# Summing the squares of a norm block by block between the tiles of the product before it

## What is computed

```python
def _rms(x, w):
    y = x * lax.rsqrt(jnp.mean(x * x, axis=-1, keepdims=True) + EPS)
    return y * w

for l in range(DEPTH):                                  # DEPTH = 2
    h = _rms(x, norm1_w[l]) * (1 + sc1) + sh1           # norm "n1"
    y = token_mixers(h)          # ends in mix @ w_o[l]: eight tiles of 128 outputs
    x = x + g1 * y
    h = _rms(x, norm2_w[l]) * (1 + sc2) + sh2           # norm "n2"
    f = swiglu(h) if l == 0 else moe(h)   # the dense one ends in a @ w_down: eight tiles
    x = x + g2 * f
```

## Time and profile before

| | us |
|---|---|
| median of 3 runs | 1893.72 |
| lowest, highest | 1891.28, 1897.60 |
| the profiled execution, device time | 1892.12 |
| its span in the trace | 1890.1 |
| PE busy in the span | 1731.4 |
| PE weight loads busy | 1536.9 |
| DVE busy | 1356.2 |
| ACT busy | 1091.5 |

### The profile page before, as it was taken

How to read it: one execution, slowest core, us unless ns; L and a number is a source line. 1 busy time by engine, 2 the same in 40 slices (tenths; PEclk the granted TensorE clock), 3 DMA queues, 4 the chain that set the end, 5 groups by cost and what they waited for, 6 DMA issues and landing times.

```text
span 1890.1 us, 33664 instructions
## 1 busy us (share of the span) xinstructions
PE 1731.4 (92%) x11984; PEld 1536.9 (81%) x11984; DVE 1356.2 (72%) x2228; ACT 1091.5 (58%) x1837; POOL 39.4 (2%) x47
## 2 busy tenths in 40 slices
PE   6997888999989887767999999999999999999995
PEld 3884457999978654556999999999999999999995
DVE  4477345454455754357889889898898988988985
ACT  4453324444344532245777777777777777777772
POOL 0000100000000000000000000000000000000000
PEclk8998898999989997688999999999999999999998
DMA  9651362445436314037999999999999999999993
GB/s 385 219 199 45 135 266 90 156 165 186 160 112 236 136 45 164 1 159 268 363 360 365 355 347 379 359 357 365 353 363 359 346 380 360 360 359 348 370 358 124
DMA packets 52272, 494.22 MB, mean 261 GB/s; under 512 B 6256, under 2 KB 6560, under 8 KB 11120
## 3 DMA queue, kind: packets, MB, share of 16 engines
q1 hardware_dynamic: 48000, 479.59, 67.3%
q0 software_dynamic: 3840, 12.57, 1.8%
q10 hardware_dynamic: 368, 1.19, 0.2%
HBM read 484.97 MB, written 8.35 MB: 261 GB/s over the span
## 4 chain that ended last, share of the span: by engine, by line
PE 86%; DVE 8%; ACT 3%; DMA 2%; issue 2%; DVEq 0%; SPq 0%; ACTq 0%; POOLq 0%
PE bank L1019 17%; PE bank L1004 11%; PE bank L1006 11%; PE bank L1005 11%; PE bank L582 7%; PE bank L584 7%; PE bank L583 7%; PE bank L618 3%; PE bank L1012 1%; PE bank L590 1%; PE bank L865 1%; PE bank L778 1%; PE bank L843 1%; PE bank L597 1%; PE bank L839 1%
## 5 line engine op out<-in xcount | busy, mean ns | idle before, releaser
L1983 DVE TENSOR_TENSOR w_lo<-xring,w_hi 128x1024 fp32r<-128x1024 f32 x448 | 528.7, 1221 | 94.3 <-ACT w_hi L1335 94.3
L1004 PE MATMUL bank<-w_hi,hg_hi 128*128 128x256 f32 x1792 | 510.2, 285 | 5.6 <-DVE w_lo L1983 2.9
L1006 PE MATMUL bank<-w_hi,hg_lo 128*128 128x256 f32 x1792 | 507.9, 283 | 0.0
L1005 PE MATMUL bank<-w_lo,hg_hi 128*128 128x256 f32 x1792 | 507.7, 283 | 0.0
L1335 ACT ACTIVATE w_hi<-xring 128x1024 fp32r<-128x1024 f32 x448 | 449.7, 1060 | 0.0
L1004 PEld LDWEIGHTS bank<-w_hi,hg_hi 128*128 128x128 f32 x1792 | 342.1, 191 | 17.9 <-DVE w_lo L1983 4.7
L1005 PEld LDWEIGHTS bank<-w_lo,hg_hi 128*128 128x128 f32 x1792 | 342.1, 191 | 7.5
L1006 PEld LDWEIGHTS bank<-w_hi,hg_lo 128*128 128x128 f32 x1792 | 342.3, 191 | 0.0
L1983 DVE TENSOR_TENSOR wd_lo<-xring,wd_hi 128x1024 fp32r<-128x1024 f32 x224 | 273.0, 1219 | 0.0
L1338 ACT ACTIVATE wd_hi<-xring 128x1024 fp32r<-128x1024 f32 x224 | 236.5, 1056 | 2.1 <-PEq L973 2.1
L1351 ACT ACTIVATE sgX<-bank 128x128 f32<-128x128 f32 x224 | 62.2, 278 | 252.2 <-PE bank L1006 252.2
(11 more groups left out here) (305 smaller groups left out, 2613.5 us busy)
## 6 DMA issues: line engine op xcount, KB each, us to landing
xring<-w_moe SPq DMA_DIRECT2D x224, 1536.0 KB, 8.6
ring<-w_ada SPq DMA_DIRECT2D x32, 1536.0 KB, 7.7
ring<-w_win SPq DMA_DIRECT2D x22, 1024.0 KB, 6.6
ring<-w_up SPq DMA_DIRECT2D x22, 1024.0 KB, 4.8
ring<-w_down SPq DMA_DIRECT2D x8, 1408.0 KB, 5.9
ring<-w_wo SPq DMA_DIRECT2D x8, 1024.0 KB, 6.3
ring<-w_wqb SPq DMA_DIRECT2D x2, 1152.0 KB, 8.6
ring<-w_wkvb SPq DMA_DIRECT2D x2, 1024.0 KB, 5.5
```

Source lines behind the costliest of these rows:

```text
L1004: mm(banks[j][:, 0:256], hg_hi[:, k], w_hi[:, j % 2, cols], start=k == 0, stop=False)
L1005: mm(banks[j][:, 0:256], hg_hi[:, k], w_lo[:, j % 2, cols], start=False, stop=False)
L1006: last = mm(banks[j][:, 0:256], hg_lo[:, k], w_hi[:, j % 2, cols], start=False, stop=k == KD - 1)
L1983: v.tensor_tensor(lo, xring[:, s + D * p:s + D * p + D], hi.bitcast(F32), ALU.subtract).then_inc(sem("lo_done"), 1)
```

## The change

`SS_LAG = 2` is new. On PE, block k - 2 of the sum of squares is multiplied right behind tile k, for k from 2 on; behind the last tile come the last three blocks. On ACT, the square of a block stands behind the rounding of a later tile's weights. The eight blocks accumulate in one bank, which is taken at tile 2 instead of after tile 7. In the bank plan the sum therefore comes at another place, and the n1 of layer 1 gets a stated bank (3) and no longer takes a turn. DVE, SP and POOL keep their instructions in their order.

```diff
@@ psum_plan
-        use(("ss", l, "n1"))
         if l == 0:
+            use(("ss", l, "n1"))
             ada(("start", 0))
...
         for k in range(KD):
             use(("wo", l, k))
-        use(("ss", l, "n2"))
+            if k == SS_LAG:
+                use(("ss", l, "n2"))
         if l == 0:
             plan["before the dense layer"] = list(count)
             for k in range(KD):
-                use(("down", k), (4 + k) % 8)
+                use(("down", k), (4 + k) % 8 if k < KD - 1 else 4)
+                if k == SS_LAG:
+                    use(("ss", 1, "n1"), 3)
@@ PE
-            def sum_x_squares(l, name):
-                o = use(("ss", l, name))
-                for k in range(KD):
+            def sum_x_squares(l, name, ks=range(KD)):
+                o = use(("ss", l, name)) if ks[0] == 0 else ps(("ss", l, name))
+                for k in ks:
                     pe.wait_ge(sem("x_squared"), KD * (2 * l + (name == "n2")) + k + 1)
                     last = mm(o[:, 0:T], ones, sq8_f[:, k * T:(k + 1) * T], start=k == 0, stop=k == KD - 1)
-                full(last, ("ss", l, name))
+                if ks[-1] == KD - 1:
+                    full(last, ("ss", l, name))
+
+            def sum_behind(l, name, k):
+                if k >= SS_LAG:
+                    sum_x_squares(l, name, range(k - SS_LAG, KD if k == KD - 1 else k - SS_LAG + 1))
...
                 for k in range(KD):
                     tile_product((NP + KD) * l + NP + k)
-                sum_x_squares(l, "n2")
+                    sum_behind(l, "n2", k)
...
                         full(last, ("down", k))
+                        sum_behind(1, "n1", k)
@@ ACT
                 for k in range(2, KD):
                     round_weights((NP + KD) * l + NP + k)
-                square_x(l, "n2", (sem("x1_ready"), KD * l))
+                    if k > SS_LAG:
+                        square_x(l, "n2", (sem("x1_ready"), KD * l), [k - SS_LAG - 1])
+                square_x(l, "n2", (sem("x1_ready"), KD * l), range(KD - SS_LAG - 1, KD))
...
                     for d in range(2, KD * DOWN_PIECES):
                         round_down_piece(d)
+                        if d >= SS_LAG * DOWN_PIECES and d % DOWN_PIECES == 1:
+                            square_x(1, "n1", (sem("ffn_x_ready"), 0), [d // DOWN_PIECES - SS_LAG])
```

More of the change, by code:

```diff
@@ L187 @@
 MLA_ORDER = mla_order()
+SS_LAG = 2
 def psum_plan():
@@ L629, in _ @@
                     modulation(("start0", 0))
-                sum_x_squares(l, "n1")
                 if l == 0:
+                    sum_x_squares(l, "n1")
                     modulation(("start", 0))
@@ L1087, in modulation_rows, with square_x @@
                     act.sem_inc(sem("modrow_ready"), 1)
-            def square_x(l, name, ready):
-                for k in range(KD):
+            def square_x(l, name, ready, ks=range(KD)):
+                for k in ks:
                     act.wait_ge(ready[0], ready[1] + k + 1)
                     A(sq8_f[:, k * T:(k + 1) * T], xT[:, k * T:(k + 1) * T], ACT.Square).then_inc(sem("x_squared"), 1)
-                act.sem_inc(squares_ready, 1)
+                if ks[-1] == KD - 1:
+                    act.sem_inc(squares_ready, 1)
             def shift_rounded(l, dst, col, k, signal):
@@ L1119, in _ @@
                     act.wait_ge(sem("eps_ready"), 1)
-                square_x(l, "n1", (sem("xT_ready"), 0) if l == 0 else (sem("ffn_x_ready"), 0))
                 if l == 0:
+                    square_x(l, "n1", (sem("xT_ready"), 0))
                     modulation_rows(("start0", 0))
+                else:
+                    square_x(l, "n1", (sem("ffn_x_ready"), 0), range(KD - SS_LAG, KD))
                 finish_norm(l, "n1", D)
```

## The result

| | before | after |
|---|---|---|
| median (lowest to highest), us | 1893.31 (1889.82 to 1897.60) | 1896.88 (1893.86 to 1901.24) |
| profiled execution, device time | 1892.12 | 1895.26 |
| its span | 1890.1 | 1893.2 |

The ratio is 1.0023 [1.0016, 1.0030], so the change costs 4.4 us (3.0 to 5.7); the medians differ by 3.6 us. That is within the 0.3% that a single measurement tells from no change. With 22 runs on each side it is a small, real loss, larger than the +1.8 us forecast. The runs of either kernel lie in two groups (before 18 up to 1894.0 us and 4 from 1895.8 on, after 15 up to 1898.2 and 7 from 1899.9 on), and their medians differ by 3.3 us in the lower groups and 3.5 in the upper ones. The two profiled executions differ by 3.1 us in both time and span, so their traces can account for most of it.

The account below looks back on a forecast made before the run. PE, busy 92% of the span, was taken as the bound. Both w_o places +1.9, down product -0.75 and bank wait +0.6 us gave +1.8, so 1895.5 us against the median of 1893.7; range 1890.0 to 1899.3 us.

Parts of the forecast that it names:

- The class: Whole kernel: no difference beyond 0.3%, 5.7 us; same was given 0.90, faster 0.05, slower 0.05.
- Tails: Sum of squares behind three products: logarithm 2.29 us after the tile's end instead of 4.14, 5.55 us saved in all.
- Blocks between tiles: Both w_o products: five blocks at 0.56 us each, less the 1.85 us shorter tail, +0.95 us per place.
- the edge: PE, switching between a block and fp32r tiles: 0 to 0.17 us extra per block, taken as 0.08.
- the modulation step: Nearest rows with fp32 matmuls after a tile: 0.09 us over pitch going over, 0.08 going back.
- Down product: Five blocks between pieces cost net 0.22 us each, less the 1.85 us shorter tail: -0.75 us.
- the weight hole: Down product, at tile starts: PE loses 0.34 us waiting for weights, which a block would fill.
- Bank plan: Layer 1: head 0's scores wait for ACT's copy of tile 21 from bank 4, +0.6 us, or 0 if hidden.
- Squares on ACT: ACT's squares in w_o and the down product fall into its waits and cost nothing on the path.
- The clock: PE restarts at half clock after idle time; shifted restarts were allowed 1 us either way.
- The signs that the prediction named for being wrong: w_o tiles keeping their 3.20 us pitch, an edge over 0.3 us, or a changed length of the expert part.

Follow-up runs that it names:

- a run of its own: The changed kernel with layer 1's projection given back its earlier PSUM banks; 1896.56 us, ratio 1.0011 to the kernel before.
- the direct remedy: The changed kernel plus four redundant matmuls keeping PE busy ahead of layer 1's router; 1897.86 us, ratio 1.0014 to the kernel before.
- the one trace with all of them: Kernel before with all three sums three tiles behind and redundant matmuls in seven PE waits; 1888.15 us, ratio 0.9979 to the kernel before.

## Why the prediction came out as it did

The class was right (no difference beyond 0.3%), the range held the median, and the sign of +1.8 us was right. The size was short by about 2.6 us of 4.4. That the sign came out right is mostly luck: the terms that the sum was made of came to +0.4 us, not +1.8, and a term that was only allowed for, either way, brought the rest.

- *Tails*: 2.29 us predicted, 2.28 and 2.28 measured. Right in the sum, with two small errors that cancel. The last block began 1.43 us after the tail did (310.13 - 308.70) and not 1.50, for PE followed the square's end (309.64 + 0.44) by 0.05 us and not 0.12; from there to the logarithm it was 0.85 us and not 0.79. The wait before it shows as 0.30 us and not half a microsecond.
- *Blocks between tiles*: pitch 3.76 predicted, 3.67 measured. The step that failed is the edge: the 0.08 us taken from the modulation step is not there. 0.467 us is less than the bare 0.48 used, so w_o cost 0.47 and not 0.95 a place.
- *Down product*: pitch 9.36 predicted, 9.27 measured, for the same reason; -1.2 us instead of -0.75. That the block fills the weight hole was right.
- *Bank plan*: 0.6 predicted, 0.55 of idle time measured, gone in a run of its own. Right. The 0.8 in its stretch is no better than the scatter of that stretch.
- *Squares on ACT*: free, as said.
- *The clock*: the step that failed most. "For three restarts, not all one way, I allow 1 us either way" was argued from a shift of a restart by a microsecond. What moved was not the restart. The router of layer 1 began at 825.2 in both traces; the stretch at 1.2 GHz was 3.4 us long in one and 6.8 in the other. That made +3.1 us with the ranking behind it, all in one direction. The prediction had looked at the clock only behind layer 0's w_o, where it was low in any case, and not at the router, where two matmul groups stood half inside such a stretch and so had something to lose. The signs that the prediction named for being wrong (the tiles' pitch, the edge, the length of the expert part) all stayed quiet; none looked at router and ranking.

The own terms came to +0.4 us, less than predicted; the clock to +3.1. Together that is 3.5 of the 4.4 us, and of the 3.1 us between the profiled executions all but what the scatter elsewhere gave back. The remaining microsecond is within the interval, and the 3.6 us between the medians leave nothing over. That the router's clock carries the loss is shown in three traces with the long stretch against five with the short one. That the medians would fall by it is not shown, since the direct remedy met another loss of clock.

The Trainium skill (TensorE: Matmul & The Clock Gate, Why this matters for your kernels) advises against idle gaps of TensorE between bursts of matmuls beyond a length that the 2.74 us ahead of the router stay under. The clock fell in eight of the ten traces with this gap, so the traces don't bear out that a gap shorter than that is safe.

## What to carry to other kernels

Move work out of a tail only as long as what remains still covers the last dependency: four blocks of eight stayed free here, a fifth cost its full 0.47 us between the tiles. When an edit touches the work just ahead of an idle gap, read the granted clock behind that gap and price the next matmuls at both levels, for the clock can swallow several times what the edit itself moves. Where PE waits anyway, a few redundant matmuls can be worth more than the reordering, but read the granted clock of the whole program again behind such an edit: in the one trace with all of them a fall lay in the ranking and cost 0.9 us.

## What the runs showed of the hardware

- Plain fp32 matmuls between fp32r tiles cost nothing beyond their own time: 0.467 us for two of 288 columns, in w_o; the modulation step had suggested otherwise.
- The granted clock fell 1.5 to 2.3 us into an idle gap of 2.74 us, or, in two executions, not at all, and stayed low for either 3.4 or 6.8 us. The same sixteen matmuls took 4.84 us at the upper level, 5.39 to 5.50 with the short stretch and 6.78 to 6.85 with the long one.
- The place of the fall followed an earlier fall (75.1 us behind the one in attention, in all eight traces), not the moment at which PE went idle.
- One kernel's times lay in two groups, 1889.7 to 1891.2 and 1896.1 to 1898.5 us, in the twelve runs of one comparison.
